# The last output projections of each sub-layer tile by tile, begun inside the recurrent mixer's last periods, in a two-layer encoder on eight cores

## The reference

```python
D_MODEL = 1024; BATCH = 16; SEQ = 2048; DEPTH = 2
CHUNK = 64; HG_HEADS = 8; MEM_LEN = 256; X_HEADS = 4; D_FF = 2816

def rmsnorm(x, g):
    xf = x.astype(jnp.float32)
    y = xf * lax.rsqrt(jnp.mean(xf * xf, axis=-1, keepdims=True) + EPS)
    return (y * g.astype(jnp.float32)).astype(x.dtype)
...
    for i in range(DEPTH):
        h = rmsnorm(x, norm_mix[i])
        if i % N_MIXERS == 0:
            y = short_conv_mixer(h, conv_w_in[j], conv_w[j], conv_w_out[j])
        else:
            y = hgrn2_mixer(h, hgrn_w_in[j], hgrn_w_out[j], hgrn_norm[j], lb_all[i])
        x = x + y
        h = rmsnorm(x, norm_xattn[i])
        x = x + memory_cross_attn(h, rmsnorm(mem, norm_mem[i]), xattn_w_q[i], xattn_w_kv[i], xattn_w_o[i])
        h = rmsnorm(x, norm_ffn[i])
        x = x + swiglu(h, ffn_w_in[i], ffn_w_out[i])
    return rmsnorm(x, final_norm)
```

## Time and profile before

| | us |
|---|---|
| median of 3 runs | 3894.43 (3894.36 to 3895.82) |
| profiled execution, device time | 3893.89 |
| profiled execution, span of the slowest core (core 2) | 3892.1 |
| spans of the 8 cores | 3888.1 to 3892.1 |
| PE, DVE, ACT, POOL busy, of the span | 3663.6, 1827.6, 1368.7, 470.1 |

### The profile page before, as it was taken

One profiled execution on the slowest core, in us unless ns is written; L12 is line 12 of the kernel. 1 busy time (PEld: TensorE's weight loads), 2 busy tenths in 40 slices (PEclk: granted clock), 3 DMA queues, 4 the chain that ended last, 5 costly groups with the idle time before them and its releaser, 6 DMA issues.

```text
span 3892.1 us, 54148 instructions; the slowest of 8 cores (3888.1 to 3892.1 us)
## 1 busy us (share of the span) xinstructions
PE 3663.6 (94%) x18832; PEld 1772.2 (46%) x18832; DVE 1827.6 (47%) x2708; ACT 1368.7 (35%) x2435; POOL 470.1 (12%) x664
## 2 busy tenths in 40 slices
PE   6999999998887999999999999999988879999997
PEld 2444444444554544444434544444445535444443
DVE  4554522326777543313475544323377765523224
ACT  3235411015775453010342453010267745520102
POOL 0002100001444020000000020000024431200000
PEclk9999999999998999999999999999999989999998
DMA  5435023221120521222465521232312116022322
GB/s 132 66 62 80 12 33 44 34 43 22 24 43 18 87 39 22 34 43 36 84 184 76 87 44 22 33 44 33 44 21 35 23 33 103 6 33 33 44 33 87
DMA packets 43704, 192.40 MB, mean 49 GB/s; under 512 B 2864, under 2 KB 7088, under 8 KB 25520
## 3 DMA queue, kind: packets, MB, share of 16 engines
q0 software_dynamic: 20160, 146.81, 25.4%
q1 hardware_dynamic: 23280, 42.14, 3.4%
HBM read 318.96 MB, written 16.78 MB: 86 GB/s over the span
## 4 chain that ended last, share of the span: by engine, by line
PE 82%; DVE 8%; ACT 4%; issue 4%; DMA 1%; POOL 0%; DVEq 0%; SPq 0%; ACTq 0%; POOLq 0%
PE ps L513 31%; PE ps L413 20%; PE ps L459 8%; PE ps L669 5%; PE ps L757 5%; PE ps L624 5%; PE ps L354 2%; DVE gqk_sb L856 1%; DVE F_sb L809 1%; DVE hT_sb L367 1%; ACT B_sb L348 1%; ACT L842 1%; PE ps L793 1%; PE ps L570 1%; DVE xT_sb L367 1%
## 5 line engine op out<-in xcount | busy, mean ns | idle before, releaser
L513 PE MATMUL ps<-hT_sb,slot 128*128 128x512 bf16 x5632 | 1218.2, 379 | 0.0
L513 PEld LDWEIGHTS ps<-hT_sb,slot 128*128 128x128 bf16 x5632 | 551.1, 98 | 664.5
L413 PE MATMUL ps<-aT_sb,slot 128*128 128x512 bf16 x3840 | 838.3, 380 | 3.7 <-DVE aT_sb L970 2.4
L519 ACT ACTIVATE F_sb<-ps 128x512 f32<-128x512 f32 x352 | 210.2, 597 | 1410.8 <-PE ps L513 1400.1
L521 DVE TENSOR_TENSOR aT_sb<-ps,F_sb 128x512 bf16<-128x512 f32 x352 | 243.0, 691 | 938.2 <-PE ps L513 925.0
L413 PEld LDWEIGHTS ps<-aT_sb,slot 128*128 128x128 bf16 x3840 | 375.9, 98 | 458.7 <-issue 9.6
L417 DVE TENSOR_TENSOR xT_sb<-ps,xT_sb 128x512 f32<-128x512 f32 x512 | 347.3, 690 | 392.2 <-PE ps L413 388.1
L757 PE MATMUL ps<-hT_sb,slot 128*128 128x512 bf16 x1536 | 368.6, 386 | 40.1 <-ACT F_sb L769 30.0
L1208 POOL DMA_DIRECT2D slot<-wp x140 | 76.0, 543 | 2265.3 <-PE ps L513 1219.4
L367 DVE SCALAR_TENSOR_TENSOR hT_sb<-xT_sb,cst_sb,F_sb 128x512 bf16<-128x512 f32 x368 | 287.2, 781 | 129.3 <-ACT F_sb L362 99.8
L459 PE MATMUL ps<-hT_sb,slot 128*128 128x512 bf16 x1536 | 338.1, 383 | 5.2 <-DVE hT_sb L367 2.9
(11 more groups left out here) (103 smaller groups left out, 2888.9 us busy)
## 6 DMA issues: line engine op xcount, KB each, us to landing
slot<-wp POOLq DMA_DIRECT2D x140, 1024.0 KB, 10.9
outT<-xT_sb SPq DMA_DIRECT2D x8, 2048.0 KB, 8.3
xT_sb<-xT SPq DMA_DIRECT2D x7, 2048.0 KB, 14.1
F_sb<-memT SPq DMA_DIRECT2D x4, 1024.0 KB, 9.5
xT_sb<-xT SPq DMA_DIRECT2D x8, 256.0 KB, 11.7
hT_sb<-xT SPq DMA_DIRECT2D x1, 2048.0 KB, 17.2
F_sb<-xT SPq DMA_DIRECT2D x1, 2048.0 KB, 23.3
F_sb<-ctab SPq DMA_DIRECT2D x1, 128.0 KB, 2.2
```

The lines of the kernel that those rows point to most:

```text
L413: P.pe(lambda e, kc=kc, mo=mo, pb=pb, ts=ts: e.matmul(psb[pb][:], lhsT=slot[:, kc, mo * 128:(mo + 1) * 128], rhs=aT[:, kc, ts], start=(kc ...
L513: P.pe(lambda e, kc=kc, pb=pb, co=co, ts=ts: e.matmul(psb[pb][:], lhsT=slot[:, kc, co:co + 128], rhs=hT[:, kc, ts], start=(kc == 0), stop= ...
L519: P.act(lambda e, pa=pa, fs=fs: e.activation(out=Fp[fs], in_=psb[pa][:], func=AF.Silu), reads=[("ps", pa)], writes=[("F", fs)])
```

## The change

1. **The last pair of output pieces goes tile by tile.** Both pieces are held (`held`), and class `OutNorm` does a tile in four quarters of two output chunks. A quarter emits its matmuls and evictions, a part of the norm of the tile before, and the squares of its own two chunks. The norms alternate between two sets of buffers for the squares. The last tile's sums and multiplications stay deferred.
2. **After the recurrent mixer** these quarters stand inside periods 14, 15 and 16 (`drain`), for tiles 0, 1 and 2, where unit n+2's projections stood in earlier periods; tile 3 follows the last period.
3. **In the convolution** the norms of tiles 2 and 3 are cut in two: squares after units 5 and 9, sums and multiplications after units 6 and 10. `hT` has one token for each tile and chunk now, so a matmul waits for its own chunk.
4. **The final norm** gives odd chunks to POOL (a multiplication by the root) and ACT (a multiplication by the gain). At the end of the program the last tile is stored in four parts.
5. **At the start** the first weight piece waits for tile 0, tile 1 for that piece; tile 1 is normed behind the first unit. The convolution's pieces are loaded with 384 columns instead of 512.
6. **At the change of sequence** tile 2 is loaded early too (into `aT`), and the full tiles in the order 3, 0, 1, 2. Of layer-0 and layer-1 attention, half of the copies of K and of the folded matrix move from ACT to DVE.
7. In the recurrent mixer's first periods the deferred norm is spread over two periods.

```diff
+    class OutNorm:
+        def trail(self, tt, q):
+            nm = self.norm[tt]
+            if q == 1:
+                nm.sums()
+            elif q > 1:
+                nm.apply(range(4 * q - 8, 4 * q - 4))
+                if q == 3 and self.after is not None:
+                    self.after(tt)
+
+        def quarter(self, tt, q):
+            out_quarter(self.held, self.nkc, tt, q)
+            if tt > 0:
+                self.trail(tt - 1, q)
+            self.norm[tt].squares((2 * q, 2 * q + 1))
+            if (tt, q) in self.extra:
+                self.extra[(tt, q)]()
...
+                if self.shared and c % 2 == 1:
+                    P.pool(lambda e, out=out, src=src: e.tensor_tensor(out=out, in0=src, in1=self.root, op=ALU.mult),
+                           reads=[self.reads(c), self.rtok], writes=[self.writes(c)])
+                    P.act(lambda e, out=out, g=g: e.activation(out=out, in_=out, func=AF.Copy, scale=g),
+                          reads=[self.writes(c), "cst"], writes=[self.writes(c)])
+                    continue
...
+        def drain(n, pos):
+            if n < NU - 2 or pos not in (0, 2, 3, 5):
+                return
+            if not tail:
+                held = (take(), take())
+                spec = lambda tt: norm_x(g_next, tt, (8, 9, 8, 10)[tt], (TH3, TH2, TH3, TB)[tt])
+                tail["out"] = OutNorm(held, 8, spec, extra=mem_parts(l))
+            tail["out"].quarter(n - NU + 2, (0, 2, 3, 5).index(pos))
+
         for n in range(-2, NU + 1):
             period(n)
+            if n == NU - 2:
+                free(2)
+            if n == NU - 1:
+                xa_mem(seq)
+        for q in range(4):
+            tail["out"].quarter(NT - 1, q)
+        tail["out"].close()
...
-        load_tile(seq, 1)
+        refill(reads=[xtok(c, 0) for c in range(8)], limit=1)
+        load_tile(seq, 1, reads=[("slot", 0)])
         refill(reads=[xtok(0, 1)])
         for tt in range(2, NT):
             load_tile(seq, tt, reads=[("slot", 3)])
-        for tt in range(2):
-            norm_one("g_mix0", tt)
+        norm_x("g_mix0", 0, 9).whole()
...
-                        after = {0: flush, 5: (lambda: norm_one("g_mix0", 2)), 9: (lambda: norm_one("g_mix0", 3))}
+                        after = {0: flush if seq > 0 else (lambda: norm_x("g_mix0", 1, 10).whole()),
+                                 5: lambda n2=n2: n2.squares(range(8)),
+                                 6: lambda n2=n2: (n2.sums(), n2.apply(range(8))),
+                                 9: lambda n3=n3: n3.squares(range(8)),
+                                 10: lambda n3=n3: (n3.sums(), n3.apply(range(8)))}
...
-                out=slot[:].rearrange("p a b -> p (a b)"), in_=wpd[pi]), reads=list(reads), writes=[("slot", k % NSLOT)])
+                out=slot[:, :, 0:nw], in_=wpd[pi].rearrange("p (a b) -> p a b", b=512)[:, :, 0:nw]), reads=list(reads), writes=[("slot", k % NSLOT)])
```

More of the change, by code:

```diff
@@ new lines, in build_program, with __init__, all, close @@
+    class OutNorm:
+        def __init__(self, held, nkc, spec, after=None, extra=None):
+            self.held, self.nkc, self.after, self.extra = held, nkc, after, extra or {}
+            self.norm = [spec(tt) for tt in range(NT)]
+        def trail(self, tt, q):
[13 more added lines that the diff above has]
+                self.extra[(tt, q)]()
+        def all(self):
+            for tt in range(NT):
+                for q in range(4):
+                    self.quarter(tt, q)
+        def close(self):
+            tt = NT - 1
+            self.norm[tt].defer(None if self.after is None else (lambda: self.after(tt)))
@@ L615, in xa_stage @@
         nout = {"n": 0}
+        xnorm = [norm_x(g_next, tt, 10 if tt < NT - 1 else 9) for tt in range(NT)]
         def scores(k, between=None):
@@ L1197, in build_program @@
+    width = [384 if kind == "conv_in" else 512 for lp in pcs for (kind, _, _) in lp]
     order = []
@@ L1232, in build_program @@
     sems = {k: es.enter_context(nc.semaphore("s_" + "_".join(str(x) for x in k))) for k in P.semkeys}
[L1233 removed]
+    fw = [(k, v) for k, v in P.final_counts.items() if k[0] == "dma" and k[1][:2] in ("ou", "oc")]
     with nc.Block() as block:
```

343 lines of the change are left out of this document (191 added, 152 removed).

## The result

The changed kernel takes 0.9892 of the time before (95% interval 0.9863 to 0.992); ratios below are to the kernel before as well. Its profiled execution took 3852.11 us (3893.89 before): 41.8 us won, where 71 were forecast. The direction held. The time lies in the stated range (3797 to 3855), but near its edge and outside the forecast's own case (3803 to 3843), and most terms of the sum did not hold. The slowest core is now core 3.

The account below looks back on a forecast made before the run. PE was taken as the bound, busy 3663.6 of 3892.1 us, so only its waits and low-clock stretches could be won. Terms: 32 + 16 + 1 + 3 + 4 + 10 + 5 = 71; 3893.9 - 71 = 3823 us, range 3797 to 3855.

Parts of the forecast that it names:

- the mixer's end: Recurrent mixer's last periods, with projection quarters inside them: 16 us won each, 32 in all; bounds 8 and 26 each.
- the locking rival: Queues lock each other in the recurrent mixer's added periods: 4 us won at each end and start, 3855 us; chance 0.2.
- The ledger: Count of DVE's work at the mixer's end: DVE sets its length, attention begins at 1304.7 instead of 1321.8, 17 us.
- DVE does not hold PE up: PE's floor decides the mixer's end, 25 us won each, and 12 at each mixer start; about 3797 us; chance 0.12.
- the low clock stays: Short waits keep PE at 1.2 GHz through the mixer's end: attention 48 us later, twice; 3951 us; chance 0.04.
- The mixer's start: Recurrent mixer's start, norms by tiles: of 13 us lost, 8 won each, 16 in all; bounds 3 and 12.
- Start: Program's start, first loads one after the other: 76.3 us against 79.2, 3 us won; bounds -4 and 7.
- Convolution's norms: Norms cut in two at four places in the convolution: 1 us won in all; bounds -4 and 16.
- Change of sequence: Between the two sequences, half of the final norm goes to POOL: 4 us won; bounds -8 and 7.
- The rival in which the start and the change of sequence both lose: Small-run loads take twice as long and POOL blocks DVE: -4 and -8 instead of 7; 3838 us; chance 0.07.
- End: Last projection matmul to the program's end: 16 us instead of 25.2, 10 won with earlier transfers; bounds 7 and 13.
- Attention's copies: Copies shared between ACT and DVE: about 1.2 us at each of four attentions, 5 in all; bounds 0 and 8.

Follow-up runs that it names:

- Experiment 1: The changed kernel with the recurrent mixer's output projection put back behind the last period instead of inside the last three: 3880.2 us, ratio 0.9962.
- experiment 8: The changed kernel with ACT's squares of each projected quarter one quarter later in the recurrent mixer's end: 3836.1 us, ratio 0.9852.
- experiment 10: The changed kernel with the edits of experiment 6, Experiment 7, experiment 8 and experiment 9 together: 3804.1 us, ratio 0.9757.
- experiment 11: The changed kernel with attention's copies shared as before the change and the convolution's norms of tiles 2 and 3 whole behind units 5 and 9: 3869.0 us.
- experiment 5: The changed kernel with the loads that wait for tile 1 asked for behind the first unit's instructions at the program's start: 3849.2 us, ratio 0.9883.
- experiment 6: The changed kernel with first weights asked for at half of tile 0, tile 1's squares ahead of unit 0, other loads behind it: 3844.7 us.
- Experiment 7: The changed kernel with the memory's norm a quarter of a tile earlier at the ends of the convolution and the recurrent mixer: 3843.2 us.
- experiment 4: The changed kernel with the final norm's multiplications all on DVE, none on POOL and ACT: 3848.2 us, ratio 0.9881.
- experiment 9: The changed kernel with the final norm shared for the very last tile only and the next sequence's first two norms two quarters earlier: 3840.5 us.
- experiment 2: The changed kernel with the convolution's weights loaded with their padding, in runs of 512 columns: 3851.4 us.

## Why the prediction was right, and where its terms were off

The forecast got the direction and, by its main mechanism, the mixer's end right. That the time fell into the range is in part luck: 3852 us is 29 above the forecast and 3 below the price of the locking rival, whose terms were not right either (it had 4 us at each mixer's end and 4 at the starts, where 10.5 each and 25.8 were won).

**The mixer's end (32, measured 21.0): right mechanism, wrong bound.** Experiment 1 shows the win is that of the quarters in the periods. The ledger's first step was near (the first multiplication of `powers` on DVE begins at 1214.91 in period 14 and at 1239.75 in period 15: 24.8 us, forecast 23.3). Its end was not: the K matmuls begin 88.4 us after the first of these, against the ledger's 83.0, and with the same work for DVE 79.8 in experiment 8 and 77.2 in experiment 10. DVE was busy for 70% of the stretch, where over 85% was to show that it sets the end. So "DVE sets this" is refuted. The change showed 16.4 us of PE idle beside 27 of DVE idle in that stretch: neither engine's total set its length, but their order. The rival of locking queues was right on what happens (squares wait for evictions, copies for squares) and its price of 12 us each was near what undoing it gives back (9.5 and 10.2 in experiment 8). Only some 5 us each are missing against the ledger, because without the lock 20 each were to be had and not the ledger's 16. The rival "DVE does not hold PE up" described what was to be had, 23 of its 25, once the lock was gone. The bound of 26 each by PE's floor was not passed.

**The clock there.** "I expect 2.4 GHz" was nearly right: 0.96 over the stretch, 16 matmuls at the lower level after two waits of over 2.4 us. One of the prediction's signs of being wrong, a clock that falls between the quarters, did so turn up, at one place, and cost some 2.4 us there (6.03 instead of 3.6). The rival "the low clock stays" did not occur, and PE waited for no piece of weights in attention.

**The mixer's start (16, measured 25.8): mis-sized.** Of the 13 us lost there before, 11.7 were won in the first sequence and 14.1 in the second, where 8 was said. What was mis-sized is the 5 us of the 13 that the sum left in place, naming only ACT's changes of table. ACT changes its table more often now (five loads of 1.28 us from 913 to 930), but DVE kept up, as "just even" said, and PE's only wait over 0.1 us from 890 to 945 is 1.2 us. This is the largest win of all, and it is read from the traces alone: no experiment undoes the order by tiles in the feed-forward stage, or the deferred norm's spreading over two periods, so what each is worth stays open. Of the two sequences' wins 5.7 each lie ahead of the mixer's first matmul, 6.1 and 8.5 behind it.

**Start (3 won, measured some 7 lost: 2.9, and 3.9 that experiment 11 gives the norms there).** The sum had tile 0 at 9.5 us and tile 1 at 25.5; on core 3 the loads that wait for these tiles begin at 13.36 and 34.46, and unit 0 at 23.39. It also left out POOL's queue: it spoke of pieces that "come one after the other", not of what stands behind their issue. The memset there costs 3.7 us by experiment 5. The rest is the order of transfers, of which experiment 6 gets 3 more back; what the best order would be stays open, since unit 1's start differs between cores by 5 us in the same run.

**Convolution's norms (1): 5.0 by experiment 11.** The waits for late chunks came as said, but add up to 3.6 us over two places (13 waits of at most 0.3 us), where the sum had 3.3 to 5 at each.

**Not in the sum: 5.5 us at the convolution's output projections.** The memory's norm was moved into their last quarters and costed only in the mixer's ledger. PE waits 2.4 us for it on core 3. Experiment 7 wins back more than was lost.

**Change of sequence (4 won, measured some 7 lost).** That POOL's multiplications would delay DVE by more than they save was named as what would break the term. They took back all that they saved: over the whole program DVE's 32 remaining multiplications of the final norm take 42.4 us, and all 64 take 43.5 in experiment 4. By the Trainium skill (GPSIMD Engine Reference, Key points) POOL contends with DVE instructions that have two SBUF inputs. The trace agrees, with 1.76 us for such a multiplication beside POOL's and 0.68 in a row without it. On top of that come ACT's scaling copies, which wait for POOL. Together this is 6 us (experiment 4); how they share it was not tried. The place of the next sequence's norms, worth as much again (5.7 us, experiment 9), was not in the working.

The rival in which the start and the change of sequence both lose (chance 0.07) had -4 and -8, and some 7 were lost at each. Half of its reason held: POOL blocked DVE, but the narrow loads took no longer than full ones (experiment 2). Its time is added up wrongly: with -12 instead of 7 the sum is 52, and 3893.9 - 52 = 3842 us, not 3838.

**End (10, measured 5.1).** From PE's last projection matmul to the end are 17.7 us on core 3 (3832.9 to 3850.6), 7.5 fewer than on core 2 before, where the sum had 16. In the mean of the cores 6.3 us are won there and 1.3 lost ahead of it, in the last feed-forward stage, for a reason that stays open. DVE's four multiplications beside POOL's take 6.86 us, as counted (7.0). Late were the last squares, 2.43 us of PE's wait, behind the same scaling copies.

**Attention's copies (5, measured 4.1).** Close by chance. Split up, attention won 8.6 us where PE waited for the copies, from the folded matrix to the first matmul of `xa_vw` (mean of the cores, all four), and lost 4.5 in the 64 K matmuls at its head. These follow a wait that is new, and run partly at the lower clock behind it. Second attention's K matmuls, before and with the change (columns as in the earlier trace rows):

```profile
1321.76:1330.10 8.34, 7.15 (x65) 6.19 (x64) 7.71 (x12) 7.55 (x14) 1.05 (x2) 1.00 0.86 126
1303.27:1313.10 9.83, 8.81 (x64) 7.06 (x65) 3.89 (x6) 1.78 (x3) 1.00 (x2) 0.83 0.82 125
```

So the late norm of the memory costs once more behind its own stage, and experiment 7, which takes the wait away, has these matmuls at 7.15 us again.

So the forecast held because the range took in errors of both signs: 11 us less at the mixer's ends than forecast, 10 more at its starts, and 28 less in the other stages, most of them where a new order of queues cost what it should have won.

## What to carry to other kernels

Where several engines each have idle time in a stretch and it is still long, no total bounds it: look at what stands behind each instruction that waits, on its own in-order queue, above all cheap ones that wait for another engine (squares for evictions, loads for a tile). Put such an instruction a step later than where its input is made; that alone doubled the win of the mixer's end here. Of work moved into another stage, write down every stage that it enters, for the one left out of the ledger is the one that pays.

## What the runs showed of the hardware

- A casting load of 768 KB in rows of 384 columns takes as long as one of 1024 KB in full rows (10.1 and 10.2 us), and POOL spends 0.87 us on its issue instead of 0.53.
- After a wait of 3.5 us the 64 K matmuls run at a granted clock of 0.83 and take 8.81 us of PE's time, and 7.15 at 1.00.
- DVE's multiplication of two inputs in SBUF takes 0.68 us alone in a row of four and 1.7 beside POOL's: here its last four beside POOL's last four, then all of the final norm's on DVE, shared (change) and not shared (experiment 4).

```profile
3839.26 6.86 DVE L383 SCALAR_TENSOR_TENSOR xT_sb<-xT_sb,cst_sb,F_sb 128x512 f32<-128x512 f32 x4 [2.70 <-ACT F_sb L370]
3839.30 6.27 POOL L378 TENSOR_TENSOR xT_sb<-xT_sb,F_sb 128x512 f32<-128x512 f32 x4 [4.14 <-ACT F_sb L370]
...
L383 DVE SCALAR_TENSOR_TENSOR xT_sb<-xT_sb,cst_sb,F_sb 128x512 f32<-128x512 f32 x32 | 42.4, 1368 | 9.9 <-ACT F_sb L370 9.9
L383 DVE SCALAR_TENSOR_TENSOR xT_sb<-xT_sb,cst_sb,F_sb 128x512 f32<-128x512 f32 x64 | 43.5, 745 | 7.5 <-ACT F_sb L370 7.3
```

- The time to a core's second unit at the program's start, where eight cores load at once, differs by some 5 us between cores of one run (46.1 on core 3, 40.9 on core 0), more than several of the edits tried there are worth.
